# Clearing two DRAM buffers from SyncE's queue in the midst of layer 0's attention in place of GpSimd's, and a later start for GpSimd's gate products

## The chip, the cores and the metric

One core of one Trainium2 chip runs the whole program. The metric is the time of one execution on the device in microseconds (us); of several runs the median counts.

## The reference, cut to what matters

A trunk of two layers works on 512 tokens of 1024 features. Each layer has a mixer, whose three head groups read one normalised input, and a channel mixer: a dense SwiGLU in layer 0, a mixture of 8 experts with 2 chosen per token in layer 1. What matters here is the recurrent head group, whose result is multiplied by a gelu of `y`, and the fact that the experts need rows of memory that are cleared beforehand.

```python
def recurrent_group(x_in, y_in, conv_w, conv_b, wa, ba, wx, bx, lam):
    xc = causal_conv(x_in, conv_w, conv_b)
    return rg_lru(xc, wa, ba, wx, bx, lam) * jax.nn.gelu(y_in)

def mixer(...):
    a_out = recurrent_group(x_lru, y_lru, ...)
    b_out = mla_group(...)            # 6 heads, causal attention
    c_out = nsa_group(...)            # 6 heads, selected and window attention
    return jnp.concatenate([a_out, b_out, c_out], axis=-1) @ w_out

def moe_ffn(x, router_w, wg, wu, wd):
    ...                               # each token goes to its 2 best experts
```

## The kernel before, in words

TensorE (PE), VectorE (DVE), ScalarE (ACT), GpSimd (POOL) and SyncE (SP) each run one list of instructions, written by hand in program order and tied together by semaphores: `signal(...)` raises one, `ready(...)` is what another engine waits for.

**A layer** begins with a stage of projections and small preparatory steps (the table PREPARE), then comes attention, then the output projection (rows with `xT` of DVE line L2316), then the channel mixer. Weights come in chunks of 512 KB: SP loads chunk J into one of two buffers `wstage` (L2544) after DVE has split chunk J-2 (L1885), ACT rounds it into `wring_hi` (L1546), DVE forms the rest `wring_lo` (L1885), and PE multiplies. A chunk can be split only when PE has finished with the chunk three places earlier. In layer 0 the last chunks of the loop, the eight of the output projection, are therefore loaded partly during attention and partly after it.

**Attention** is a series of steps s, each with one or two blocks of 128 query rows for two heads; steps of pairs are named (pair, block of rows). The first steps are (0,1), then (0,0) with (0,2), then (0,3), then (1,3). For each step, by engine:

- PE: `scores(s)`, products of queries and keys (L1387) and the causal mask (L1392); then, for the step three back, transposes of the probabilities (`turn`, L1405) and, when a pair is complete, products with the values (L1435; L1424 those of the compressed keys). `scores(s)` waits for ACT's exponentials of step s-2, `turn` waits for DVE's scaling of its step.
- DVE: `scale(s-2)`, a reciprocal (L2227), a product with the gates (L2238) and one multiplication by a per-row factor for each block (L2245, in place); then `maximum(s)`, a reduction of the scores (L2213 to L2220) that raises the semaphore `nmx`.
- ACT: copies of the transposed blocks to SBUF (L1750), then `exps(s)`, the exponentials (L1739), which wait for `nmx` of step s.

Both `scale(0)` and the maxima of steps 0 and 1 belong to the end of the preparatory stage. From step 2 on each engine walks through the steps in order. The maximum of the fourth step, s = 3, comes after `scale(1)` on DVE, and `scale(2)` follows it.

**GpSimd** has little to do. In each layer it issues four pairs of small transfers (L2482, L2483), then, for the two halves c of `y`, three elementwise products that prepare the gelu: `y*y` (L2489, two inputs), a scaling with an added constant (L2491, one input) and a product with `y` (L2493, two inputs). They wait for `y` and for the scan of the recurrence. ACT takes the results in its steps 7 and 8 of attention (`gelu_tanh`, L1684), DVE finishes the recurrence from its step 9 on. After these products GpSimd issues, in layer 0 alone, the transfers that clear DRAM: ten into `expert_results` (L2499) and nine into `expert_slots` (L2505). Their source is one zeroed piece of SBUF, 256 numbers a partition of `iota`, read again and again. The first waits for `nmx` of step 0. The rest of GpSimd's list are squares of `xT` in the output projection (`early_squares`, L2459 to L2468), and in layer 1 the scatter of tokens into `expert_slots` (L2520), which waits until everything is cleared.

```python
if l == 0:
    pool.wait_ge(*ready("nmx", l, 0, 0))
    ...
pool.wait_ge(*ready("lru_out", l, LC - 1))
...
early_squares((l, "ffn"), lambda k: ready("x_mixed", l, k), l == 1)
```

**SyncE** issues nearly all other transfers, in program order. In the loop over chunks of layer 0 it waits, before each chunk, for the split of the chunk two earlier; between chunks stand small transfers that swap halves of rotated vectors (L2557). During attention itself it has only chunks left. In layer 1 it reloads `iota` after all clearing has landed.

Of the kernel before, what the change touches and what calls it, by code (L numbers as in the profile page):

```python
# [29 lines left out]
P = 128  # L30
T = 512
TT = T // P
DM = 1024
# [18 lines left out]
NE = 8  # L52
# [26 lines left out]
NF = len(FEAT)  # L79
# [90 lines left out]
def trunk(nc, io, known):  # L170
    with ExitStack() as ctx:
# [903 lines left out]
        def experts_sp(sp):  # L1075

            def store(n):
                sp.wait_ge(M["turned"], TURNED[n + 1])
                for h, w in row_halves(CAPS[n]):
                    a = n * YROWS + h * P  # L1080
                    sp.dma_start(results_dram[a:a + w, :], ystage[0:w, h, :]).then_inc(M["stored"], 16)

            def load_rows(n):


                sp.wait_ge(*ready("blank", "slotted"))
                if n >= 4:
                    sp.wait_ge(M["gather_mm"], (n - 1) * KC)
                for h, w in row_halves(CAPS[n]):
                    a = n * YROWS + h * P  # L1090
                    sp.dma_start(slot_rows[n % 2][0:w, h, :],
                                 slots_dram[a:a + w, :]).then_inc(*signal(f"wstage{n % WS}", "slots", n, by=16))

            def chunk_of(expert, f):
                return io["ew"][bass.ds(expert * FC + f, 1)].rearrange("a p n -> p (a n)")

            sp.wait_ge(*ready("order"))
            for G in range(NG):
                n, f = divmod(G, FC)
                if f == 0:  # L1100
                    expert = sp.value_load(order[0:1, n:n + 1], min_val=0, max_val=NE - 1)
                if G == 2:
                    sp.wait_ge(*ready("tok_h", TT - 1))
                    sp.wait_ge(*ready("tok_l", TT - 1))
                if G >= ES:

                    sp.wait_ge(M["lo_ready"], FC + max(G - ES, 1) + 1)
                if G < 2:
                    for p in ((0, 1, 2), (3, 4))[G]:
                        _, part, loaded_ = first_part(p)  # L1110
                        sp.dma_start(ew[:, G, part], chunk_of(expert, G)[:, part]).then_inc(loaded_, 16)
                else:
                    sp.dma_start(ew[:, G % ES, :], chunk_of(expert, f)).then_inc(ew_loaded[G % ES], 16)
                if f == 1 and n >= 2:
                    store(n - 2)
                if f == 3 and n + 1 >= 2 and n + 1 < NE:
                    load_rows(n + 1)
            store(NE - 2)
            sp.wait_ge(M["stored"], STORED[NE - 1])
            sp.wait_ge(*ready("flag"))  # L1120
            over = sp.value_load(flag[0:1, 0:1])
            with sp.If(over > 0):
                sp.wait_ge(M["lo_ready"], FC + NG)
                with sp.Fori(1, ROUNDS) as r:
                    for e in range(NE):
                        n = r * NE + e
                        expert = sp.value_load(order[0:1, e:e + 1], min_val=0, max_val=NE - 1)
                        for f in range(FC):
                            sp.wait_ge(M["lo_ready"], n * FC + FC + last_in(ES, f) + 1)
                            sp.dma_start(ew[:, f % ES, :], chunk_of(expert, f)).then_inc(ew_loaded[f % ES], 16)  # L1130
                        sp.wait_ge(M["turned"], turned_again(n) + NTA)
                        for h, w in row_halves(CAP):
                            sp.dma_start(results_dram[bass.ds(r * CAP + (e * YROWS + CAPS[e] - CAP + h * P), w), :],
                                         ystage[0:w, h, :]).then_inc(M["stored"], 16)
                sp.wait_ge(M["stored"], STORED[NE - 1] + 16 * NHA * (ROUNDS - 1) * NE)
            sp.sem_inc(M["all_stored"], 1)
# [1310 lines left out]
        def _(pool):  # L2447
# [22 lines left out]
            for l in range(DEPTH):  # L2470
                if l > 0:
                    early_squares((l, "mix"), lambda k: (D["y_added"], KC * HALVES + k + 1))

                for s, src in enumerate((kcT, vcT)):
                    if s == 0:
                        pool.wait_ge(*ready("roped", l, "kc", 0))
                    else:
                        pool.wait_ge(*ready("feat", l, feat_index("vc", 0)))
                        pool.wait_ge(*ready("win", l, 0))
                    for g in range(2):  # L2480
                        rows = src[g * HD:(g + 1) * HD, :]
                        pool.dma_start(kcg[0:HD, g, :], rows).then_inc(*signal("kcg", l, s, by=16))  # L2482
                        pool.dma_start(kcg[HD:P, g, 0:T - 1], rows[:, 1:T]).then_inc(*signal("kcg", l, s, by=16))  # L2483
                for c in range(LC):

                    y, u = yl[:, c, :], tmp[:, 2 + c, :]
                    pool.wait_ge(*ready("feat", l, feat_index("y", c)))
                    pool.wait_ge(*ready("lru_step", "scan", l, c))
                    pool.tensor_tensor(u, y, y, ALU.mult).then_inc(*signal("gelu_in", l, c, 0))  # L2489
                    pool.wait_ge(*ready("gelu_in", l, c, 0))  # L2490
                    pool.tensor_scalar(u, u, 0.044715, 1.0, ALU.mult, ALU.add).then_inc(*signal("gelu_in", l, c, 1))  # L2491
                    pool.wait_ge(*ready("gelu_in", l, c, 1))
                    pool.tensor_tensor(u, u, y, ALU.mult).then_inc(*signal("gelu_in", l, c, 2))  # L2493
                if l == 0:
                    pool.wait_ge(*ready("nmx", l, 0, 0))
                    blank = results_dram.rearrange("(p a) d -> p (a d)", p=P).rearrange("p (a n) -> p a n", n=256)
                    for a in range(0, blank.shape[1], 16):
                        n = min(16, blank.shape[1] - a)
                        pool.dma_start(blank[:, a:a + n, :], iota[:, 0:256].unsqueeze(1).broadcast_to([P, n, 256])  # L2499
                                       ).then_inc(*signal("blank", by=16))  # L2500
                    for e in range(2, NE):
                        rows = slots_dram[e * YROWS:e * YROWS + CAPS[e], :].rearrange("r (a n) -> r a n", n=256)
                        for a in range(0, CAPS[e], P):
                            w = min(CAPS[e] - a, P)
                            pool.dma_start(rows[a:a + w], iota[0:w, 0:256].unsqueeze(1)  # L2505
                                           .broadcast_to([w, DM // 256, 256])).then_inc(*signal("blank", by=16))
                pool.wait_ge(*ready("lru_out", l, LC - 1))
                if l == 1:
                    pool.wait_ge(*ready("x_mixed", l, 0))
                    pool.wait_ge(*ready("late_consts"))  # L2510
                    pool.tensor_copy(lowerb, lower[:, :]).then_inc(*signal("counters"))
                    pool.tensor_copy(onesb, ones[:, :]).then_inc(*signal("counters"))
                early_squares((l, "ffn"), lambda k: ready("x_mixed", l, k), l == 1)
            pool.wait_ge(*ready("rows"))
            pool.wait_ge(*ready("blank"))
            for i in range(TT):
                pool.wait_ge(*ready("tok_h", i))
                pool.wait_ge(*ready("tok_l", i))
                for at in (0, TT):
                    pool.indirect_dma_start(slots_dram, bass.IndirectOffsetOnAxis(  # L2520
                        ap=row_index[:, at + i:at + i + 1], axis=0), tok_[:, i, :], None
                        ).then_inc(*signal("blank", "slotted", by=16))
            pool.wait_ge(M["all_stored"], 1)
            pool.wait_ge(M["gather_mm"], NE * KC)
            for i in range(TT):
# [11 lines left out]
        def _(sp):  # L2537
# [9 lines left out]
            def swap_halves(l, n):  # L2547
# [7 lines left out]
                for a in range(0, src.shape[0], 2 * half):  # L2555
                    for x, y in ((a, a + half), (a + half, a)):
                        sp.dma_start(swap[at + x:at + x + half, n % 2, :], src[y:y + half, :]  # L2557
                                     ).then_inc(*signal(f"swapped{n % 2}", l, n, by=16))

            def spread_kpe(l):  # L2560

                sp.wait_ge(*ready("roped", l, "kpe", 0))
                sp.dma_start(kh[NOPE:DQK, :, :], kpe[NOPE:DQK, :].unsqueeze(1).broadcast_to([ROPE, HEADS, T])
                             ).then_inc(*signal("spread", l, "kpe", by=16))
# [19 lines left out]
            for l in range(DEPTH):  # L2584
                for J in range(NW * l + (WR + 1 if l == 0 else WS), NW * (l + 1)):
# [7 lines left out]
                    for n, (name, c) in enumerate(ROPES):  # L2593
                        if j == (1 if name == "kpe" else feat_index(name, c)) + WS + WR:
                            swap_halves(l, n)
                    if j == 4 + WS + WR + 1:
                        spread_kpe(l)
                    if 0 <= j - (5 + WS + WR + 1) < 2:
# [188 lines left out]
```

## Time and profile before

| what | value |
|---|---|
| median of 3 runs | 1330.28 us (1328.93 to 1330.73) |
| the profiled execution, its own time | 1324.21 us |
| its span in the profile | 1322.4 us |
| mean granted TensorE clock, as a share of 2.4 GHz | 0.989 |
| busy: PE, DVE, ACT, POOL | 1267.1, 949.1, 677.8, 130.1 us |
| layer 0: attention | about 128 to 221 us |
| layer 1: attention | about 726 to 816 us |
| moved by DMA | 260.26 MB |

Times in rows are us from the start of the span. A row of a timeline has the start, the duration, the engine, the line, the operation and what ended the idle time before it. A granted clock of 1.00 is 2.4 GHz and 0.50 is 1.2 GHz; a value between them is a mean over a stretch in which both occurred.

### The profile page before, as it was taken

What the parts mean: (1) busy time and instruction counts of PE and PEld (TensorE: products, weight loads), DVE (VectorE), ACT (ScalarE), POOL (GpSimd) and SP (SyncE); (2) the same over time, 40 slices, a digit from 0 to 9 for tenths busy, and PEclk for the clock granted to TensorE, in tenths of its full rate; (3) what the DMA queues carried; (4) which work ended last, traced back from release to release, by engine and by line L of the source; (5) the groups of instructions that cost most, each with busy time, mean ns of one, the idle gap of its engine ahead of it and who ended that gap; (6) DMA issues with size and microseconds to landing.
All of it is one profiled execution on the core that took longest, in us unless ns stands there. A gap on an engine that the chain in (4) does not pass through costs nothing.

```text
span 1322.4 us, 24758 instructions
## 1 busy us (share of the span) xinstructions
PE 1267.1 (96%) x10314; PEld 819.6 (62%) x10375; DVE 949.1 (72%) x1304; ACT 677.8 (51%) x993; POOL 130.1 (10%) x113
## 2 busy tenths in 40 slices
PE   7999999999999999999999999979999999999992
PEld 3457565444444444444457565569979988989981
DVE  7886885886531556334886885688788799989996
ACT  6256774443210333112265774365586687787772
POOL 0011320600000000031011000501200000000002
PEclk9999899999999999999999999999999999999997
DMA  8551881444310443012551000168999999999975
GB/s 272 184 151 35 317 334 60 146 186 149 118 67 0 150 165 148 0 33 103 194 150 35 20 1 21 61 238 325 360 381 376 349 348 398 374 352 398 359 307 208
DMA packets 43134, 260.26 MB, mean 197 GB/s; under 512 B 6522, under 2 KB 7546, under 8 KB 28554
## 3 DMA queue, kind: packets, MB, share of 16 engines
q1 hardware_dynamic: 33626, 224.77, 46.1%
q0 software_dynamic: 8960, 33.26, 7.0%
q8 instruction: 84, 1.38, 0.4%
q10 hardware_dynamic: 432, 0.59, 0.1%
q14 instruction: 32, 0.26, 0.1%
HBM read 218.00 MB, written 33.65 MB: 190 GB/s over the span
## 4 chain that ended last, share of the span: by engine, by line
PE 84%; issue 6%; DVE 4%; DMA 3%; POOL 1%; ACT 1%; SPq 0%; POOLq 0%; DVEq 0%; ACTq 0%
PE bank L1177 20%; PE bank L1178 20%; PE bank L1179 19%; PE bank L1387 5%; PE bank L1435 3%; PE bank L1405 3%; PE bank L727 1%; PE bank L726 1%; PE bank L725 1%; DMA expert_slots<-arena,row_index 1%; PE bank L735 1%; PE bank L737 1%; PE bank L736 1%; POOL expert_slots L2520 1%; PE bank L1242 1%
## 5 line engine op out<-in xcount | busy, mean ns | idle before, releaser
L988 DVE SCALAR_TENSOR_TENSOR arena<-arena 128x3072 f16<-128x3072 f32 x86 | 288.2, 3352 | 10.8 <-ACT arena L842 9.1
L842 ACT ACTIVATE arena<-arena 128x3072 f16<-128x3072 f32 x86 | 237.9, 2767 | 41.1 <-DMA arena<-in_ew 19.5
L1177 PE MATMUL bank<-arena 128*128 128x144 bf16 (+3 forms) x877 | 215.1, 264 | 6.0 <-DVE arena L988 2.7
L1178 PE MATMUL bank<-arena 128*128 128x144 f16 (+3 forms) x878 | 215.4, 264 | 0.1
L1179 PE MATMUL bank<-arena 128*128 128x144 bf16 (+3 forms) x867 | 211.2, 263 | 0.0
L1178 PE MATMUL bank<-hl,wring_hi 128*128 128x512 f16 x352 | 133.4, 379 | 1.5 <-issue 0.6
L1179 PE MATMUL bank<-hh,wring_lo 128*128 128x512 bf16 x341 | 129.2, 379 | 0.0
L1177 PE MATMUL bank<-hh,arena 128*128 128x512 bf16 x338 | 128.1, 379 | 1.0
L1178 PE MATMUL bank<-hl,arena 128*128 128x512 f16 x338 | 128.1, 379 | 0.0
L1177 PE MATMUL bank<-hh,wring_hi 128*128 128x512 bf16 (+1 forms) x333 | 126.3, 379 | 1.0 <-DVE wring_lo L1885 0.5
L1179 PE MATMUL bank<-hh,arena 128*128 128x512 bf16 x319 | 120.9, 379 | 0.0
L1177 PE MATMUL bank<-wring_hi,arena 128*128 128x112 bf16 (+1 forms) x704 | 113.6, 216 | 1.5 <-DVE arena L988 1.5
L1179 PE MATMUL bank<-wring_hi,arena 128*128 128x112 bf16 (+1 forms) x704 | 113.5, 216 | 0.0
L1178 PE MATMUL bank<-wring_lo,arena 128*128 128x112 f16 (+1 forms) x704 | 113.4, 216 | 0.0
L1546 ACT ACTIVATE wring_hi<-wstage 128x1024 f16<-128x1024 f32 x44 | 46.4, 1056 | 116.9 <-PE bank L1179 76.2
L1177 PEld LDWEIGHTS bank<-arena 128*128 128x128 f16 x878 | 85.9, 98 | 30.9 <-DVE arena L988 3.2
L1178 PEld LDWEIGHTS bank<-arena 128*128 128x128 f16 x878 | 85.9, 98 | 22.8 <-issue 0.3
L1179 PEld LDWEIGHTS bank<-arena 128*128 128x128 f16 x878 | 85.9, 98 | 22.4
L1739 ACT ACTIVATE arena<-bank,small 128x256 f32<-128x256 f32 (+3 forms) x144 | 75.1, 545 | 23.7 <-DVE small L2220 13.7
L1562 ACT ACTIVATE arena<-arena 128x512 f32<-128x512 f32 x22 | 13.9, 630 | 135.1 <-DVE arena L1921 135.1
L725 PE MATMUL bank<-arena 128*128 128x144 bf16 (+2 forms) x352 | 74.2, 233 | 2.5 <-DVE arena L1021 2.5
L726 PE MATMUL bank<-arena 128*128 128x144 f16 (+2 forms) x352 | 74.2, 233 | 0.0
(334 smaller groups left out, 2521.2 us busy)
## 6 DMA issues: line engine op xcount, KB each, us to landing
arena<-in_ew SPq DMA_DIRECT2D x86, 1536.0 KB, 9.1
arena<-in_dw SPq DMA_DIRECT2D x22, 1536.0 KB, 6.4
wstage<-in_w_chunk SPq DMA_DIRECT2D x44, 512.0 KB, 3.9
expert_results<-iota POOLq DMA_DIRECT2D x9, 2048.0 KB
arena<-in_cmp_w SPq DMA_DIRECT2D x2, 2048.0 KB, 8.0
arena<-arena SPq DMA_DIRECT2D x60, 64.0 KB, 2.1
expert_slots<-iota POOLq DMA_DIRECT2D x5, 512.0 KB
expert_results<-wstage SPq DMA_DIRECT2D x5, 512.0 KB
```

The costliest lines, as they stand in the source:

```text
L725: pe.matmul(out, hi, a_hi, start=(first and m % 2 == 0), stop=False, skip_group_check=True)
L726: pe.matmul(out, hi, a_lo, start=False, stop=False, skip_group_check=True)
L842: act.activation(ew_hi_[:, G % EP, :], ew[:, G % ES, :], ACT.Copy, scale=SW).then_inc(M["hi_ready"], 1)
L988: dve.scalar_tensor_tensor(out=ew_lo_[:, G % EP, :], in0=ew[:, G % ES, :], scalar=SW, in1=ew_hi_[:, G % EP, :], op0=ALU.mult, op1=ALU.subt ...
L1177: pe.matmul(out, w_hi, x_hi, start=first, stop=False)
L1178: pe.matmul(out, w_hi, x_lo, start=False, stop=False)
L1179: return pe.matmul(out, w_lo, x_hi, start=False, stop=last)
L1387: pe.matmul(score_bank[(2 * s + ab) % 4][:, offset(s, n):offset(s, n + 1)], q, k, start=(n == 0), stop=False)
L1405: mm = pe.transpose(turn_bank[ab][:, offset(s, n) + kb * P:offset(s, n) + (kb + 1) * P], Pt[u % 2][:, ab, OFF[i] + kb * P:OFF[i] + (kb + 1 ...
L1435: mm = pe.matmul(ob[ab * HD:(ab + 1) * HD, kb * P:T], v, turned_row(u % 2, ab, kb), start=(kb == 0 and kind == "mla"), stop=(closes and last))
L1546: act.activation(wring_hi[:, J % WR, :, :], wstage[:, J % WS, :, :], ACT.Copy, scale=SW).then_inc(*signal("w_hi", J))
L1739: act.activation(Pt[u % 2][:, ab, OFF[i]:OFF[i] + (i + 1) * P], score_bank[(2 * s + ab) % 4][:, offset(s, n):offset(s, n + 1)], ACT.Exp, b ...
```

## The change

Three edits. SyncE issues the nineteen clearing transfers, in a new function `clear_rows`, after chunk 17 (counted in the order of layer 0) and ahead of the wait for chunk 18. They wait only for the zeros, which are written at the start of the program. GpSimd no longer issues them. And GpSimd's gelu products, in both layers and for both halves, wait in addition for `nmx` of step 3. The scatter's transfers raise a semaphore of their own, `slotted`, instead of sharing `blank`.

```diff
             def load_rows(n):
-                sp.wait_ge(*ready("blank", "slotted"))
+                sp.wait_ge(*ready("slotted"))
...
                 for c in range(LC):
                     y, u = yl[:, c, :], tmp[:, 2 + c, :]
+                    pool.wait_ge(*ready("nmx", l, 3, 0))
                     pool.wait_ge(*ready("feat", l, feat_index("y", c)))
                     pool.wait_ge(*ready("lru_step", "scan", l, c))
                     pool.tensor_tensor(u, y, y, ALU.mult).then_inc(*signal("gelu_in", l, c, 0))
...
-                if l == 0:
-                    pool.wait_ge(*ready("nmx", l, 0, 0))
-                    blank = results_dram.rearrange("(p a) d -> p (a d)", p=P).rearrange("p (a n) -> p a n", n=256)
-                    for a in range(0, blank.shape[1], 16):
-                        n = min(16, blank.shape[1] - a)
-                        pool.dma_start(blank[:, a:a + n, :], iota[:, 0:256].unsqueeze(1).broadcast_to([P, n, 256])
-                                       ).then_inc(*signal("blank", by=16))
-                    for e in range(2, NE):
-                        ...
                 pool.wait_ge(*ready("lru_out", l, LC - 1))
...
+            def clear_rows():
+                sp.wait_ge(*ready("by_pool", "zeros"))
+                blank = results_dram.rearrange("(p a) d -> p (a d)", p=P).rearrange("p (a n) -> p a n", n=256)
+                for a in range(0, blank.shape[1], 16):
+                    n = min(16, blank.shape[1] - a)
+                    sp.dma_start(blank[:, a:a + n, :], iota[:, 0:256].unsqueeze(1).broadcast_to([P, n, 256])
+                                 ).then_inc(*signal("blank", by=16))
+                for e in range(2, NE):
+                    rows = slots_dram[e * YROWS:e * YROWS + CAPS[e], :].rearrange("r (a n) -> r a n", n=256)
+                    for a in range(0, CAPS[e], P):
+                        w = min(CAPS[e] - a, P)
+                        sp.dma_start(rows[a:a + w], iota[0:w, 0:256].unsqueeze(1)
+                                     .broadcast_to([w, DM // 256, 256])).then_inc(*signal("blank", by=16))
...
                     for n, (name, c) in enumerate(ROPES):
                         ...
+                    if l == 0 and j == NF + WR + 1:
+                        clear_rows()
...
                     chunk(J)
```

GpSimd's list in layer 0, from its last gelu product to the squares of the output projection. Before, with what each instruction waits for:

```order
L2489 TENSOR_TENSOR arena<-arena 128x512 [waits lru_step,feat]
L2491 TENSOR_SCALAR arena<-arena 128x512 [waits gelu_in]
L2493 TENSOR_TENSOR arena<-arena 128x512 [waits gelu_in]
L2499 DMA expert_results<-iota 128x16x256 [waits nmx]
L2499 DMA expert_results<-iota 128x16x256 x8
L2499 DMA expert_results<-iota 128x4x256
L2505 DMA expert_slots<-iota 512x1x256
L2505 DMA expert_slots<-iota 160x1x256
```

And with the change:

```order
L2490 TENSOR_TENSOR arena<-arena 128x512 [waits lru_step,feat,nmx]
L2492 TENSOR_SCALAR arena<-arena 128x512 [waits gelu_in]
L2494 TENSOR_TENSOR arena<-arena 128x512 [waits gelu_in]
L2459 TENSOR_TENSOR arena<-xT 128x512 [waits x_mixed,lru_out]
L2463 TENSOR_TENSOR arena<-xT 128x512 [waits x_mixed]
```

The transfers are gone from this list, and the first product of each half has one more semaphore to wait for. The lists of PE, DVE and ACT are the same as before.

SyncE's list from the last swap of halves in layer 0 to its end; `wstage<-in_w_chunk` are the chunks of weights. Before:

```order
L2557 DMA arena<-arena 32x512 [waits roped,feat]
L2557 DMA arena<-arena 32x512 x3
L2544 DMA wstage<-in_w_chunk 128x1024 [waits w_lo] x6
L2625 UNCONDITIONAL_BRANCH [waits lru_out,pv]
L2625 ISA
```

And with the change:

```order
L2532 DMA wstage<-in_w_chunk 128x1024 [waits w_lo] x2
L2554 DMA expert_results<-iota 128x16x256 [waits by_pool]
L2554 DMA expert_results<-iota 128x16x256 x8
L2554 DMA expert_results<-iota 128x4x256
L2560 DMA expert_slots<-iota 512x1x256
L2560 DMA expert_slots<-iota 160x1x256
L2560 DMA expert_slots<-iota 448x1x256
L2560 DMA expert_slots<-iota 512x1x256
L2560 DMA expert_slots<-iota 64x1x256
L2560 DMA expert_slots<-iota 512x1x256 x2
L2532 DMA wstage<-in_w_chunk 128x1024 [waits w_lo] x4
```

Two of the six chunks now come ahead of the nineteen transfers and four behind them.

## Rows read from the trace of the kernel before

**Rows 1.** The page's chain that ended last, shares of the span by engine.
```profile
PE 84%; issue 6%; DVE 4%; DMA 3%; POOL 1%; ACT 1%; SPq 0%; POOLq 0%; DVEq 0%; ACTq 0%
```
**Rows 2.** Stretches: us; PE, PEld, DVE, ACT, POOL busy; clock, DMA share, GB/s.
```profile
128.00:148.90 20.90, 18.61 (x95) 9.89 (x96) 17.07 (x34) 12.87 (x40) 13.09 (x12) 0.84 0.60 226
726.10:744.10 18.00, 16.59 (x95) 8.45 (x96) 14.75 (x34) 11.92 (x39) 4.35 (x5) 1.00 0.07 26
148.89:218.66 69.77, 69.31 (x469) 42.24 (x472) 54.27 (x131) 49.82 (x154) 9.36 (x12) 1.00 0.74 274
744.09:813.86 69.77, 69.31 (x469) 42.25 (x472) 53.66 (x131) 50.88 (x157) 0.00 (x0) 1.00 0.03 8
```
**Rows 3.** The chain of waits, layer 0, two pieces: start, us, what.
```profile
128.05 1.08 PE bank L1387 x8
...
148.89 1.33 PE bank L1435 x5
```
**Rows 4.** The chain of waits, layer 1, the same stage.
```profile
726.17 1.08 PE bank L1387 x8
...
732.82 1.28 DVE small L2238
...
734.12 1.14 DVE arena L2245 x4
...
744.09 2.09 PE bank L1435 x11
```
**Rows 5.** Timeline of layer 0, DVE and POOL at the third step.
```profile
134.69 1.27 POOL L2493 TENSOR_TENSOR arena<-arena 128x512 f32<-128x512 f32 x1
134.71 1.27 DVE L2238 TENSOR_TENSOR small<-small,arena 128x4 f32<-128x4 f32 x1
...
135.90 8.64 POOL L2499 DMA_DIRECT2D expert_results<-iota  x7
...
136.01 2.48 DVE L2245 TENSOR_SCALAR arena<-arena,small 128x128 f32<-128x128 f32 x4
```
**Rows 6.** Timeline of layer 1, third to fifth step, POOL, DVE and ACT.
```profile
730.97 1.04 POOL L2489 TENSOR_TENSOR arena<-arena 128x512 f32<-128x512 f32 x1 [3.37 <-DVE arena L1995]
...
732.10 0.62 POOL L2491 TENSOR_SCALAR arena<-arena 128x512 f32<-128x512 f32 x1
...
736.51 0.16 DVE L2238 TENSOR_TENSOR small<-small,arena 128x2 f32<-128x2 f32 x1
736.70 0.88 DVE L2245 TENSOR_SCALAR arena<-arena,small 128x512 f32<-128x512 f32 x2
...
737.50 1.28 DVE L2220 TENSOR_REDUCE small<-bank 128x2 f32<-128x256 f32 x2
...
737.77 1.07 ACT L1750 COPY arena<-bank 128x512 f32<-128x512 f32 x2
...
738.88 0.37 ACT L1739 ACTIVATE arena<-bank,small 128x128 f32<-128x128 f32 x1
```
**Rows 7.** Timeline of layer 0's output projection, DVE and POOL.
```profile
231.08 1.21 DVE L1885 SCALAR_TENSOR_TENSOR wring_lo<-wstage,wring_hi 128x1024 f16<-128x1024 f32 x1
...
231.24 1.95 POOL L2463 TENSOR_TENSOR arena<-xT 128x512 f32<-128x512 f32 x1 [2.42 <-DVE xT L2316]
232.22 1.52 DVE L2290 SCALAR_TENSOR_TENSOR arena<-xT,gains,arena 128x512 f16<-128x512 f32 x1
```
**Rows 8.** Timelines of layer 0: ACT's rounding of chunk 18, SP's chunk 17.
```profile
228.58 1.04 ACT L1546 ACTIVATE wring_hi<-wstage 128x1024 f16<-128x1024 f32 x1
...
126.71 0.33 SPq L2544 DMA_DIRECT2D wstage<-in_w_chunk  x1
```
**Rows 9.** DMA from 127 to 210 us: queue, packets, MB, share.
```profile
q0 software_dynamic: 5888, 22.78, 73.8%
```
**Rows 10.** Stretches as in Rows 2: the first clearing, and preparation in layer 1.
```profile
137.00:175.00 38.00, 36.21 (x241) 21.47 (x240) 32.73 (x79) 28.85 (x90) 7.54 (x7) 0.91 1.00 377
...
707.00:711.00 4.00, 4.00 (x24) 2.79 (x24) 2.84 (x5) 1.19 (x2) 0.00 (x0) 0.60 0.00 0
```

More of the change, by code:

```diff
@@ L2493, in _ @@
                     pool.tensor_tensor(u, u, y, ALU.mult).then_inc(*signal("gelu_in", l, c, 2))
-                if l == 0:
-                    pool.wait_ge(*ready("nmx", l, 0, 0))
-                    blank = results_dram.rearrange("(p a) d -> p (a d)", p=P).rearrange("p (a n) -> p a n", n=256)
-                    for a in range(0, blank.shape[1], 16):
-                        n = min(16, blank.shape[1] - a)
-                        pool.dma_start(blank[:, a:a + n, :], iota[:, 0:256].unsqueeze(1).broadcast_to([P, n, 256])
-                                       ).then_inc(*signal("blank", by=16))
-                    for e in range(2, NE):
[L2502 to L2506, printed above, removed]
                 pool.wait_ge(*ready("lru_out", l, LC - 1))
@@ L2521, in _ @@
                         ap=row_index[:, at + i:at + i + 1], axis=0), tok_[:, i, :], None
-                        ).then_inc(*signal("blank", "slotted", by=16))
+                        ).then_inc(*signal("slotted", by=16))
             pool.wait_ge(M["all_stored"], 1)
```

## The prediction

> **What bounds the kernel now.** I read the page's chain first: TensorE makes up 84% of it [rows 1], so a change on GpSimd and in the queues counts only where PE waits for somebody. Then the chain in order of time shows where that is near the change: at the start of attention. The two layers run the same lists there, and before the change only layer 0 has the clearing transfers, so the trace holds its own comparison. From the scores of the second step to the first products with values layer 0 takes 148.89 - 128.05 = 20.84 us [rows 3] and layer 1 takes 744.09 - 726.17 = 17.92 us [rows 4]: 2.92 us more in layer 0. In the 69.77 us behind that, the two layers are equal to the hundredth, with the DMA engines 74% busy in one and 3% in the other, and 12 of GpSimd's instructions in the one and none in the other [rows 2]. So PE hides there what DVE and ACT lose, and DMA traffic as such costs nothing. All the change can give, and take, lies in the short first stretch, where PE waits for DVE's chain: scaling, maximum, then ACT's exponentials.
>
> In that stretch three things are seen. First, in both layers DVE's tiny product L2238 (4 numbers a partition) lasts 1.27 us or 1.28 us at the third step, exactly beside GpSimd's last product L2493, which began 0.02 us earlier [rows 4, 5]; one step later the like instruction lasts 0.16 us [rows 6]. Second, in layer 0 the next four multiplications L2245 last 2.48 us while GpSimd issues clearing transfers [rows 5], against 1.14 us in layer 1 [rows 4]. Third, the granted clock is 0.84 in layer 0's stretch, so PE ran part of it at 1.2 GHz, against 1.00 in layer 1 [rows 2]; PE had stood waiting just ahead of that.
>
> **The change, part by part.**
>
> *The clearing off GpSimd.* What layer 0 loses against layer 1 goes: 2.92 us. Of it 2.48 - 1.14 = 1.34 us is the stall of four instructions; the rest are smaller stalls of the same kind and the low clock that followed the wait. I take the whole 2.92 us; the lower end is 1.3 us, if the clock falls there all the same.
>
> *The clearing on SP.* The nineteen transfers are issued right after chunk 17, at about 127.0 us [rows 8], ten us earlier than now. They move 22.78 MB [rows 9]. At the 377 GB/s of the first clearing [rows 10] that is 60 us, so they end near 187 us. SP is the only engine held up, and behind the transfers in its list stand the last four chunks. The first of them, chunk 18, is rounded by ACT at 228.58 us [rows 8]. The cover is thus 228.58 - 127.04 = 101.5 us, and the queue must keep up 22.78 / 101.5 = 224 GB/s. Priced at nothing. If the cover fails, the output projection waits for its weights (see the rivals). Attention itself needs no transfer in that time. The scatter in layer 1 waits for the clearing, which lies some 700 us earlier.
>
> *The products no longer beside the third step.* DVE's L2238 falls from 1.27 to about 0.17 us in both layers, and the maximum of step 3 comes 1.10 us earlier.
>
> *The products beside the fourth step.* They now start with that maximum. In layer 1's old times: L2238 of the next scaling starts at 736.51 us now [rows 6], so at 736.51 - 1.10 = 735.41 us then, and the maximum ends some 0.1 us ahead of it. Two engines start at once: GpSimd with L2489, 1.04 us long [rows 6], and DVE with `scale(2)`, that is L2238 of 0.16 us and two L2245 of 0.88 us together, whose end lets the maximum of step 4 begin [rows 6]. Where two such instructions meet, one waits for the whole of the other: at the output projection GpSimd's L2463 stands behind DVE's L1885 and takes 1.95 us in place of the 1.04 of its like, and DVE's L2290 in turn stands behind it and takes 1.52 us [rows 7]. The waiting engine got its turn between two instructions of the other. So DVE is held here for about one product, 1.05 us. The open question is the second product, L2491, 0.62 us [rows 6]. It starts some 0.1 us after the first ends, between DVE's two L2245. If it holds DVE as well, what is left of DVE's first L2245 runs beside its wait and the sum of the delay is about 1.47 us. L2493 then falls beside the maximum L2220, which reads PSUM; the trace shows the reduction at its usual 1.2 us beside products before, so nothing is charged.
>
> What that does to the chain: without any delay the exponentials of step 4 could start at 737.78 us, which is 738.88 - 1.10, since ACT's copies L1750 move forward too. With a delay of DVE d the maximum of step 4 ends at 737.50 + 1.28 - 1.10 + d = 737.68 + d, and they start some 0.05 us later, at 737.73 + d, or at 737.78 if that is later. They start at 738.88 us now [rows 6]. So d = 1.05 gives 738.78, a gain of 0.1 us a layer, d = 1.47 gives 739.20, a loss of 0.3 us, and d = 0 gives 1.1 us. I take the middle of the two likely ones, a loss of 0.1 us a layer; that is, the old stall at the third step is exchanged for one of the same size at the fourth. The bounds are a gain of 1.1 and a loss of 0.5 us a layer.
>
> The Trainium skill speaks against the change here (page "SBUF — State Buffer", section "Who interferes with whom"): a VectorE instruction in a two-port mode, `tensor_scalar` among them, and any GpSimd instruction exclude each other for their whole length, as do two-input VectorE instructions and GpSimd ones that read SBUF. By that rule L2491 does hold L2245, and the sum would be 2.92 - 0.6 = 2.3 us in place of 2.7. No row of this trace has a one-input GpSimd product beside such a DVE instruction.
>
> *The second half's products* follow on the first's and meet `scale(3)` and `scale(4)`, which they may hold by up to two us. By then PE has transposes and, from 744.09 us on [rows 4], the long products with values to do; it waits for nobody there, and what DVE loses stays under that cover, as in rows 2. If the cover were gone, the price would be those two us a layer. ACT takes the products' results only in its steps 7 and 8, three steps on: no cost.
>
> *The semaphore of its own* for the scatter: the last increments are the same ones. Nothing.
>
> **The sum**, for the profiled execution: 2.92 - 2 x 0.1 = 2.7 us, so 1324.21 becomes 1321.5 us. The median of the runs stands 6.07 us above that execution; nothing in the trace says why, and I carry the difference over: 1330.28 - 2.7 = 1327.6 us. 0.2% is 2.66 us here, about what a measurement of this kernel tells from no change, and the forecast lies right at that bound.
>
> **The rivals.**
>
> A. *The moved products hold nobody that matters* (GpSimd reaches them late, or DVE's small instructions slip through). Then both layers gain the 1.10 us of the third step: 2.92 + 2.20 = 5.1 us, 1325.2 us. For it: a DVE reduction from PSUM is not touched. Against it: `scale(2)` begins within a tenth of a us of the products. Chance 0.10.
>
> B. *The clock.* In layer 1 a stretch ahead of attention shows a clock of 0.60 over 4 us [rows 10]: 3.2 us at 1.2 GHz, worth 1.6 us of PE's work. Layer 0 has nothing like it at the same work. Such a stretch can go when all later work shifts by 2.7 us: gain 4.3 us, 1326.0 us, chance 0.09. Or one more can come, or the one in layer 0 can stay: gain 1.1 us, 1329.2 us, chance 0.13.
>
> C. *The change does not remove the stall*: the four slow L2245 are slow for another reason than GpSimd's issuing. Then 0 to 0.3 us, 1330.2 us. Against it: the two layers differ in nothing else. Chance 0.03.
>
> D. *Slower: SP's queue becomes the bound.* The queue has one order, and chunks 18 to 21 stand behind 22.78 MB cut into pieces of 1 KB at the source. The decisive point is 224 GB/s. At 200 GB/s the clearing ends at 127 + 114 = 241 us and chunk 18 lands at least 12.5 us after it is wanted: 1330.28 + 12.5 - 2.7 = 1340.1 us. For it: no row shows this queue with such pieces. Against it: the same addresses took 377 GB/s from the other queue. Chance 0.05.
>
> **How the numbers follow.** The forecast case has 0.60 (both signs of the second product's effect in it, so 1327.2 to 1328.0 us), and it splits about evenly at the 0.2% bound: 0.32 above, 0.28 within. Faster by over 0.2%: 0.32 + 0.10 (A) + 0.09 (B) = 0.51. Within 0.2%: 0.28 + 0.13 + 0.03 = 0.44. Slower: 0.05 (D). The range reaches from A to a little above the bad side of B, as the runs before spread over 1.8 us: 1325.2 to 1329.9 us. It leaves out D, C and the tails.
>
> **What would show it.** In the new profile's layer 0 the four L2245 ahead of the fourth step's maximum last 1.14 us and the clock is 1.00 over the first stretch; from L1387 x8 to L1435 it takes 18.0 us in both layers. L2238 at the third step lasts 0.17 us. At the fourth step L2238 or L2245 lasts a us or more too long, beside L2490. SP's transfers move from 127 to about 187 us, and chunk 18 lands before 228 us. I am wrong in the mechanism if DVE shows no stall at the fourth step, or if layer 0 stays slower than layer 1 there; wrong in the cover if ACT waits for `wstage` at the output projection.

## The result and the profile after

The changed kernel takes 1336.72 us (median of 5 runs, 1335.15 to 1337.77). The kernel before, run beside it, takes 1329.56 us (5 runs, 1328.48 to 1330.73). The ratio is 1.006, 95% interval 1.0044 to 1.0075. Slower by 7.2 us, where 2.7 us faster was forecast, and outside the range.

The two profiled spans differ by more, 12.5 us (1334.9 against 1322.4), because the profiled execution of before was a quick one. I split both spans at the same instructions: the *opening* of attention is the time from the scores of the second step (L1387 x8) to the second group of value products (the second L1435 x16), so that all that PE waits for is in it.

| stretch | before | after | difference |
|---|---|---|---|
| start to layer 0's opening | 128.05 | 127.67 | -0.4 |
| opening, layer 0 | 30.34 | 33.22 | +2.9 |
| between the openings | 567.78 | 567.83 | 0 |
| opening, layer 1 | 27.42 | 33.07 | +5.7 |
| from there to the end | 568.8 | 573.1 | +4.3 |

The last row is not taken to be the change's: a second profile of the unchanged kernel (below) has 571.9 us there, and the eight experiments' profiles lie between 570 and 575 us whether they are faster or slower than before. What remains is 8.5 us in the two openings, where the median moved by 7.2 us (5.9 to 10.0 us by the interval).

The chain of waits of the changed kernel through layer 1's opening answers to [rows 4]; columns are start, us, what:

```profile
728.72 1.07 PE bank L1387 x8
...
735.38 0.18 DVE small L2238
...
735.58 1.14 DVE arena L2245 x4
736.72 1.13 DVE small L2213
...
737.96 1.04 DVE small L2238
...
739.02 2.34 DVE arena L2245 x2
741.37 1.21 DVE small L2220 x2
...
742.66 1.03 ACT arena L1739 x4
...
743.73 2.98 PE bank L1387 x3
...
747.04 1.71 PE bank L1405 x8
748.75 1.90 PE bank L1424 x4
750.65 3.95 PE bank L1435 x16
```

Up to the maximum of the fourth step (L2213 at 736.72) everything is as forecast: L2238 is down to 0.18 us, the four L2245 last 1.14 us. Then L2238 lasts 1.04 us and the two L2245 last 2.34 us in place of 0.16 and 0.88 [rows 6]. And from 743.73 us on PE's own work is stretched: the transposes L1405 x8 take 1.71 us where they took 0.88, the values L1424 1.90 where they took 1.00. Its timeline at the fourth step shows who holds whom:

```profile
737.94 1.04 POOL L2490 TENSOR_TENSOR arena<-arena 128x512 f32<-128x512 f32 x1 [60.95 <-DVE small L2213]
737.96 1.03 DVE L2238 TENSOR_TENSOR small<-small,arena 128x2 f32<-128x2 f32 x1
...
739.02 2.34 DVE L2245 TENSOR_SCALAR arena<-arena,small 128x512 f32<-128x512 f32 x2
...
739.07 0.61 POOL L2492 TENSOR_SCALAR arena<-arena 128x512 f32<-128x512 f32 x1
739.76 1.32 POOL L2494 TENSOR_TENSOR arena<-arena 128x512 f32<-128x512 f32 x1
...
743.73 2.13 PE L1387 MATMUL bank<-arena 64*128 64x512 f32 x3 [1.59 <-ACT arena L1739]
```

The two L2245 of that row, taken by themselves (shortest, median and longest in ns, first and last start):

```profile
L2245 DVE TENSOR_SCALAR arena<-arena,small x2: 942/1212/1482, 739.0 to 739.9; 128x512 f32<-128x512 f32 x2
```

GpSimd's three products each hold DVE once: L2490 holds L2238, L2492 the first L2245 (0.94 us; it ends 0.28 us after L2492), L2494 the second (1.48 us; it ends 0.28 us after L2494). PE then waits 1.59 us in one piece. The stretches of the changed kernel, columns as in [rows 2], show the clock; the first row is layer 0 and ends in the midst of its slow piece, the other two are layer 1 before and after its clock fell:

```profile
128.00:148.90 20.90, 18.04 (x90) 9.03 (x88) 18.39 (x37) 12.95 (x40) 6.04 (x6) 0.86 1.05 370
...
738.00:743.90 5.90, 3.54 (x27) 2.57 (x26) 5.79 (x8) 3.54 (x12) 5.55 (x6) 0.98 0.00 0
743.90:754.10 10.20, 10.20 (x30) 4.16 (x32) 6.30 (x15) 6.15 (x17) 0.42 (x1) 0.51 0.17 53
```

PE was busy for 3.54 of 5.90 us, and then ran 10 us at 1.2 GHz with no wait left in them. In [rows 2] layer 1's clock in this stage was 1.00. It is no matter of one execution: the mean clock of the whole program was 0.979 to 0.981 in all five executions of the changed kernel, and 0.985 to 0.992 in the 24 of the kernel before that ran beside the last experiments.

The clearing itself went as forecast. The stretch from 126.7 us on, with DMA share and rate as the last two columns:

```profile
126.70:190.00 63.30, 60.44 (x369) 32.88 (x369) 51.87 (x121) 43.64 (x136) 6.04 (x6) 0.92 1.06 374
```

And two rows of its timelines, SyncE's issue of chunk 18 and ACT's rounding of it:

```profile
185.66 1.44 SPq L2532 DMA_DIRECT2D wstage<-in_w_chunk  x1
...
231.08 1.04 ACT L1546 ACTIVATE wring_hi<-wstage 128x1024 f16<-128x1024 f32 x1
```

The transfers run at 374 GB/s, chunk 18 is issued at 185.66 us and rounded at 231.08 us with no wait for it.

### The profile page after: what moved, and what is told of

Read it like the earlier page. It is cut to its first block, busy times and chain, and to the rows that moved or that the text cites. A ratio compares the mean times of both kernels' runs of the same rounds, so it can differ in the third digit from the quotient of the medians.

```text
span 1334.9 us, 24819 instructions
## 1 busy us (share of the span) xinstructions
PE 1281.2 (96%) x10375; PEld 823.5 (62%) x10375; DVE 951.0 (71%) x1304; ACT 678.8 (51%) x993; POOL 113.5 (9%) x94
## 4 chain that ended last, share of the span: by engine, by line
PE 85%; issue 6%; DVE 4%; DMA 3%; POOL 2%; ACT 1%; SPq 0%; POOLq 0%; DVEq 0%; ACTq 0%
PE bank L1177 20%; PE bank L1178 19%; PE bank L1179 19%; PE bank L1387 4%; PE bank L1435 3%; PE bank L1405 3%; PE bank L727 1%; PE bank L726 1%; PE bank L725 1%; DMA expert_slots<-arena,row_index 1%; PE bank L735 1%; PE bank L737 1%; PE bank L736 1%; POOL expert_slots L2508 1%; PE bank L1242 1%
## 5 line engine op out<-in xcount | busy, mean ns | idle before, releaser
L1177 PE MATMUL bank<-arena 128*128 128x144 bf16 (+3 forms) x878 | 215.5, 264 | 5.7 <-DVE arena L988 3.0
L1179 PE MATMUL bank<-arena 128*128 128x144 bf16 (+3 forms) x878 | 215.4, 264 | 0.0
L1177 PE MATMUL bank<-hh,wring_hi 128*128 128x512 bf16 x352 | 133.5, 379 | 0.5 <-DVE wring_lo L1885 0.4
L1179 PE MATMUL bank<-hh,wring_lo 128*128 128x512 bf16 x352 | 133.4, 379 | 0.0
L1179 PE MATMUL bank<-hh,arena 128*128 128x512 bf16 x338 | 128.1, 379 | 0.0
L1177 PE MATMUL bank<-hh,arena 128*128 128x512 bf16 x338 | 128.1, 379 | 0.0
L1387 PE MATMUL bank<-arena 64*128 64x256 f32 (+7 forms) x288 | 71.1, 469 | 4.2 <-ACT arena L1739 4.2
```

The costliest lines, as they stand in the source:

```text
L1177: pe.matmul(out, w_hi, x_hi, start=first, stop=False)
L1179: return pe.matmul(out, w_lo, x_hi, start=False, stop=last)
L1387: pe.matmul(score_bank[(2 * s + ab) % 4][:, offset(s, n):offset(s, n + 1)], q, k, start=(n == 0), stop=False)
```

## The experiments

Eight kernels, in two groups of four as in the order below; those of one group share their runs of the kernel before (median 1328.68 us for the first four, 1327.98 us for the last four). Opening is the stretch defined above, from each kernel's own profile.

| kernel | ratio to before, 95% interval | opening, layer 0 | layer 1 |
|---|---|---|---|
| before (first profile) | 1 | 30.34 | 27.42 |
| changed | 1.006 (1.0044 to 1.0075) | 33.22 | 33.07 |
| before again | 0.9998 (0.9987 to 1.0009) | 29.20 | 27.42 |
| clearing on SyncE alone | 0.9972 (0.9956 to 0.9989) | 27.42 | 27.43 |
| late products alone | 1.006 (1.0043 to 1.0077) | 33.36 | 33.15 |
| products at the seventh step | 0.9957 (0.9940 to 0.9973) | 27.09 | 27.10 |
| second half after the sixth step | 0.9959 (0.9941 to 0.9976) | 26.31 | 26.31 |
| changed, PE's wait filled | 0.9986 (0.9972 to 1.0001) | 28.66 | 28.65 |
| changed, short second product | one execution, 1336.06 us | 33.12 | 33.06 |
| GpSimd clears from the seventh step | 0.9975 (0.9961 to 0.9988) | 27.42 | 27.42 |

The theory after the result was: the clearing's move is good, the wait does all the harm; of the harm the larger part is TensorE's clock. Rivals: SyncE's transfers do harm; attention varies by itself.

**The kernel before again.** No edit.

> The kernel before, unchanged, for a second profile of it. Its profiled execution (1324.21 us) stood 5 us under the median of its runs, so a part of the 12.5 us between the two profiled spans has nothing to do with the change. Theory: the time is about 1329.5 us (ratio 1.000), attention looks as in the first profile (20.8 us and 17.9 us for the first stretch of the layers), and the 4 to 5 us come from behind layer 1's attention. Rival: attention itself varies from one execution to the next, and then the 8.5 us of the two attentions cannot be laid to the change.

Median 1328.32 us, ratio 0.9998. Layer 1's opening is 27.42 us to the hundredth; layer 0's is 29.20, 1.1 us less than in the first profile. The DVE stall is there again (2.48 us for the four L2245 in the chain, from 137.55 us on), but the clock stayed up:

```profile
128.00:148.90 20.90, 17.94 (x100) 8.85 (x98) 17.11 (x36) 13.04 (x42) 14.52 (x13) 1.00 0.55 200
```

So of the 2.92 us that the prediction took from layer 0, 1.8 us are DVE's stall, there in both profiles (1.34 us on the four L2245 and 0.44 us on the next two), and 1.1 us are a fall of the clock that one profile has and the other has not. Why it comes in one and not in the other, the rows do not say. The same stretch of work in the first and in the second profile, with PE as busy in one as in the other, and last what followed in the first:

```profile
134.00:140.20 6.20, 4.19 (x28) 2.56 (x26) 6.06 (x11) 2.54 (x7) 6.12 (x6) 1.00 0.39 156
135.54:141.74 6.20, 4.18 (x28) 2.55 (x26) 6.06 (x11) 2.54 (x7) 6.12 (x6) 1.00 0.39 156
140.20:147.00 6.80, 6.52 (x22) 3.87 (x23) 5.64 (x16) 6.33 (x21) 4.34 (x4) 0.50 1.02 379
```

So behind this wait the clock may fall or stay. In these two profiles the openings vary by no more than that, the time ahead of them by 1.5 us (129.59 against 128.05 us) and the time behind them by 3.1 us (571.9 against 568.8 us).

**The clearing on SyncE alone.**

```diff
                 for c in range(LC):
-                    pool.wait_ge(*ready("nmx", l, 3, 0))
                     pool.wait_ge(*ready("feat", l, feat_index("y", c)))
```

> The change without its wait: SyncE clears, GpSimd's products start as before. Theory 1 (the wait at the fourth step did all the harm, and moving the transfers is good): DVE's four L2245 in layer 0 last 1.14 us, layer 0's first stretch shrinks by 2.9 us to 17.9 us, ratio about 0.998 (2 to 3 us faster than before). Rival (SyncE's transfers themselves do harm): slower than before, layer 0's attention longer than layer 1's.

Median 1323.82 us beside 1328.68, ratio 0.9972. Both layers have the same opening now:

```profile
127.66:155.08 27.42, 26.01 (x167) 14.39 (x168) 22.01 (x53) 19.02 (x63) 4.43 (x5) 1.00 1.06 371
721.24:748.67 27.43, 26.03 (x167) 14.40 (x168) 22.03 (x53) 19.03 (x63) 4.43 (x5) 1.00 0.11 37
```

Layer 0 runs it beside saturated DMA engines (share 1.06) and layer 1 beside idle ones, in the same time. The rival falls: SyncE's transfers do no harm.

The ratio amounts to 3.7 us, and the openings explain 1.8 us of it (2.9 us against the first profile). Another 1.6 us lie between the openings, which take 566.17 us here and 567.8 us in every profile above: the slow piece ahead of layer 1's attention, 0.60 in [rows 10], is absent.

```profile
700.00:720.00 20.00, 19.92 (x168) 14.15 (x167) 15.84 (x30) 16.32 (x25) 1.17 (x1) 1.00 0.00 1
```

It is absent in the last experiment too (566.16 us) and present in the six others. Whether moving the clearing alone brings this about, or chance, two profiles do not show.

**The late products alone.** Against the kernel before:

```diff
                 for c in range(LC):
+                    pool.wait_ge(*ready("nmx", l, 3, 0))
                     pool.wait_ge(*ready("feat", l, feat_index("y", c)))
```

> The wait alone: products from the fourth step on, GpSimd still clears behind them. Theory 1: in both layers DVE is held by 2.3 us at the fourth step and the clock falls for some 10 us, so attention takes about 5.7 us longer in layer 1, and in layer 0 at least as much: 9 to 12 us slower than before, ratio 1.007 to 1.009. Rival (the harm comes from SyncE's transfers): within 2 us of before.

Median 1337.36 us, ratio 1.006, openings 33.36 and 33.15 us: the changed kernel's time without its other part. The expectation was 9 to 12 us, and it came to 8.7 us; layer 0 lost less than I added up, since GpSimd's clearing waits behind its products (its first transfer is issued at 145.03 us in this kernel) and now falls where PE waits for nobody. That also shows why the clearing's move bought nothing inside the change: the late products had already moved it out of the way.

**The products at the seventh step.** Against the changed kernel:

```diff
-                    pool.wait_ge(*ready("nmx", l, 3, 0))
+                    pool.wait_ge(*ready("nmx", l, 6, 0))
```

> The change, but the products wait for the maximum of the seventh step (s = 6) in place of the fourth. Theory 1 (what counts is whether PE waits for DVE at that point): no stall at the third or the fourth step, PE is busy with values by the seventh, so the 1.1 us of the third step are gained in both layers on top of the 2.9 us: about 5 us faster than before, ratio 0.996. Rival (a product costs wherever it meets DVE): no better than the change without its wait.

Median 1322.89 us, ratio 0.9957. The time came as expected, but not by the way that was expected. The opening shrinks by only 0.33 us against the clearing alone, not by 1.1 us. The stall of the third step is gone and one of the eighth has come, as its chain shows:

```profile
144.34 2.06 DVE wring_lo L1885
...
146.91 2.50 DVE arena L2245 x2
149.42 1.21 DVE small L2220 x2
...
150.71 1.03 ACT arena L1739 x4
...
151.78 2.04 PE bank L1387 x8
```

"PE is busy with values by the seventh" was a share of busy time, not a place in the chain. Against the first profile of before, the two openings give 3.6 us of the 5.8 us by which the medians differ (3.6 to 8.0 us by the interval). The rest is in no row, and that the ratio met the expected 0.996 may be luck.

**The second half after the sixth step.** Against the changed kernel; the first half's products start as in the kernel before:

```diff
-                    pool.wait_ge(*ready("nmx", l, 3, 0))
+                    if c == 1:
+                        pool.wait_ge(*ready("pn", l, 5, 1, 0))
```

> SyncE clears; the first half's products start as in the kernel before (there DVE stands idle for over 2 us), and only the second half's three products wait, for the end of DVE's scaling of the sixth step (s = 5), behind which DVE stood idle for 2 us and then reads PSUM. Theory 1 (a product costs only where DVE has a two-input or tensor_scalar instruction on the way to a waiting PE): the 1.1 us of the third step are gained in both layers and nothing is paid at the seventh or eighth, so 2 x 1.1 us faster than the clearing on SyncE alone, 5 to 7 us faster than before, ratio about 0.9955 or less, and up to 1.5 us better than the products at the seventh step. Rival: DVE is then late for the steps after it, and nothing is gained over the products at the seventh step.

Median 1323.86 us beside 1327.98, ratio 0.9959. The timeline of its layer 0 behind the sixth step's scaling:

```profile
148.24 0.62 DVE L2245 TENSOR_SCALAR arena<-arena,small 128x256 f32<-128x256 f32 x2
...
148.94 1.04 POOL L2491 TENSOR_TENSOR arena<-arena 128x512 f32<-128x512 f32 x1 [17.19 <-DVE arena L2245]
150.06 0.62 POOL L2493 TENSOR_SCALAR arena<-arena 128x512 f32<-128x512 f32 x1
150.77 1.28 POOL L2495 TENSOR_TENSOR arena<-arena 128x512 f32<-128x512 f32 x1
152.09 0.15 DVE L2227 RECIPROCAL small<-small 128x2 f32<-128x2 f32 x1
152.27 0.16 DVE L2238 TENSOR_TENSOR small<-small,arena 128x2 f32<-128x2 f32 x1
```

The three products fit where DVE is idle or reads PSUM (`bank` in the rows), and hold nobody. The openings are 26.31 us, 1.11 us under the clearing alone in both layers, the whole of the third step's stall. The openings put it 1.6 us ahead of the products at the seventh step; the ratios cannot tell the two apart. Both beat the two kernels of this study. The gain over the kernel before is 0.4%.

**The changed kernel with PE's wait filled.**

```diff
-SPARE = {}
+SPARE = {6: 8}
```

> The changed kernel with eight superfluous products of 128x512 (bf16) on TensorE ahead of the scores of step 6, where it stands idle for 1.6 us waiting for the exponentials; they write a bank that is cleared by the next product and change no result. Theory 2 (of the 5.7 us that layer 1's attention loses, 1.2 us are the wait and the rest is the clock, which falls to 1.2 GHz for 10 us because PE stood idle): the clock stays at 2.4 GHz, and about 4 us a layer come back, so about 8 us faster than the changed kernel, ratio to before 0.999 to 1.001. Rival (the stall itself makes all of the loss): as slow as the changed kernel or slower, ratio 1.006.

Median 1326.93 us, ratio 0.9986, its interval just reaching 1. By the ratios it is 9.8 us faster than the changed kernel, and the two openings give 9.0 us. DVE's stall is untouched (L2245 x2 takes 2.35 us) and PE's scores still wait for it; but in that wait it now does useless work, and the clock stays up, as its stretches in layer 1 show:

```profile
733.00:738.90 5.90, 5.13 (x35) 3.30 (x34) 5.76 (x10) 3.35 (x11) 5.31 (x6) 1.00 0.01 3
739.00:749.20 10.20, 10.20 (x69) 5.47 (x69) 8.62 (x21) 7.97 (x23) 0.63 (x1) 1.00 0.18 51
```

Against 3.54 of 5.90 us busy in the changed kernel it is 5.13 of 5.90, and PE gets through 69 matmuls in the next 10.2 us where it got through 30. Its chain has the same work as the last rows of the changed kernel's chain above:

```profile
739.18 1.90 PE bank L1387 x4
...
741.29 0.88 PE bank L1405 x8
742.17 1.00 PE bank L1424 x4
743.18 2.31 PE bank L1435 x16
```

These four take 6.09 us in place of 10.54. The opening falls from 33.07 to 28.65 us in layer 1: 4.4 us of its 5.65 us loss were the clock, 1.2 us the wait (28.65 - 27.42), of which about 0.1 us is the filler itself running past the gap. In all ten executions of this kernel the mean clock was 0.987 or more. So the rival falls that the stall makes all of the loss.

**The changed kernel with a short second product.**

```diff
-                    pool.tensor_scalar(u, u, 0.044715, 1.0, ALU.mult, ALU.add).then_inc(*signal("gelu_in", l, c, 1))
+                    pool.tensor_scalar(u[:, 0:8], u[:, 0:8], 0.044715, 1.0, ALU.mult, ALU.add
+                                       ).then_inc(*signal("gelu_in", l, c, 1))
```

> The changed kernel with GpSimd's one-input product (tensor_scalar) on 8 of its 512 columns, so that it is nearly gone; the scaling inside the gelu is left out for the other columns. Theory 3 (each of the three products holds DVE for its own length, the one-input one too): the first of DVE's two L2245 behind the fourth maximum no longer waits 0.46 us, the pair takes about 1.9 us or less in place of 2.35, and the exponentials of step 4 start about 0.5 us earlier. Rival (only the two-input products hold DVE): the pair still takes 2.35 us.

This kernel leaves out the scaling inside the gelu for all but 8 of the 512 columns, so its result is not the reference's; only its rows are of use, from one execution. Its timeline of layer 0 at the fourth step, DVE and POOL:

```profile
138.50 1.93 DVE L2245 TENSOR_SCALAR arena<-arena,small 128x512 f32<-128x512 f32 x2
...
138.54 0.19 POOL L2492 TENSOR_SCALAR arena<-arena 128x8 f32<-128x8 f32 x1
138.81 1.33 POOL L2494 TENSOR_TENSOR arena<-arena 128x512 f32<-128x512 f32 x1
```

The pair by itself, as for the changed kernel above:

```profile
L2245 DVE TENSOR_SCALAR arena<-arena,small x2: 520/1006/1492, 138.5 to 138.9; 128x512 f32<-128x512 f32 x2
```

The pair takes 1.93 us in place of 2.35, and all of the difference is in the first of the two (0.52 us in place of 0.94; the second takes 1.49 against 1.48): the one-input product does hold DVE for its own length, and the two-input one behind it holds the second. The opening hardly changes (33.12 and 33.06 us), since the clock falls all the same; half a microsecond less of stall is not what decides that.

**GpSimd clears, from the seventh step.** Against the kernel before:

```diff
                 if l == 0:
-                    pool.wait_ge(*ready("nmx", l, 0, 0))
+                    pool.wait_ge(*ready("nmx", l, 6, 0))
```

> The kernel before with one number changed: GpSimd issues the clearing itself, but waits for the maximum of the seventh step (s = 6) in place of the first. Theory 4 (it is the moment of GpSimd's issuing, beside DVE's scaling while PE waits, that costs layer 0 its 1.8 to 2.9 us, not the queue): as fast as the clearing on SyncE alone, ratio about 0.998, four L2245 at 1.14 us in layer 0. Rival (issuing on GpSimd costs wherever it stands): no faster than before, ratio 1.000.

Median 1325.32 us, ratio 0.9975, opening 27.42 us in both layers. The clearing on SyncE gives no more (0.9972). What cost layer 0 its time was the moment at which GpSimd issued, not the queue. As with the clearing on SyncE, 1.6 us of the gain in the profile lie between the openings.

## Why the prediction was wrong, by its own steps

**What bounds the kernel: right.** All that moved lies in the openings; between them the two kernels agree within 0.05 us.

**The clearing off GpSimd: right in kind, and 1.1 us larger than the second profile has it.** The stall of L2245 is gone. I took 2.92 us from one profile; the second profile shows 1.8 us of it without any fall of the clock. By itself the part is worth 0.28% (0.11 to 0.44%), and in its profile 1.6 us of that are the missing slow piece ahead of layer 1's attention. Rival B had named such a case, gave it 0.09, and no row tells whether it is an effect of the part or chance.

**The clearing on SP: right.** Nothing, at 374 GB/s, with over 40 us to spare. The slower rival D, the only one on that side, was the wrong one.

**The third step's L2238: right**, 0.18 us in both layers.

**The products beside the fourth step: the step that failed.** It held the delay d to be 1.05 to 1.47 us, on the ground that GpSimd's third product "falls beside the maximum L2220, which reads PSUM". It did not. The first L2245, which L2492 had delayed, ran until 739.96 us, and the third product had been issued at 739.76 us, so it had its turn between the two, and the second L2245 took 1.48 us. Measured: 0.87 us on L2238, and 2.34 - 0.88 = 1.46 us on the pair, d = 2.3 us. The maximum came behind that. By the prediction's own formula, 737.73 + 2.3 is 740.0 us, 1.2 us later than 738.88, and 1.2 us is what the filled kernel shows. Rows 7 held the pattern (the waiting engine gets its turn between two instructions); I used it for the second product and dropped it for the third. The rule of the Trainium skill (page "SBUF — State Buffer", section "Who interferes with whom"), which would hold L2245 behind the one-input product too, is borne out by the short product: 2.35 us became 1.93. I had written it down and then priced half of it.

**The clock: the term that made the size.** Rival B treated the clock as chance, one stretch of 3 us worth 1.6 us. In layer 0 of the kernel before it did fall in one profile and not in the other. In the changed kernel it is a consequence: the wait, 1.2 us longer, leaves PE busy for 3.54 of 5.90 us, the clock falls, and the 10 us behind it are PE's own work, which gives little back. It fell in both layers of all three profiles with this wait (the changed kernel, the late products alone, the short product), and in neither layer once the wait was filled. 4.4 us a layer, against 1.2 us for the wait. The prediction had counted a low clock behind a wait for the clearing (0.84 in layer 0, rows 2), but priced the new wait only by when ACT could start, and put at nothing what PE's standing idle would do to the work behind it. And the two openings together explain the result: 2 x 5.65 us lost, less the 1.8 to 2.9 us that layer 0 had lost before anyway, is 8.4 to 9.5 us, near the measured 7.2 us and the 8.7 us of the late products alone.

**The second half's products: right enough.** They held `scale(3)` by about a microsecond, and nothing in the chain shows it.

What stays open: why the 570 us behind layer 1's opening vary by up to 6 us from profile to profile, and what brings or removes the slow piece ahead of layer 1's attention. No run here was aimed at either.

## What to carry to other kernels

When a helper engine's work is moved, follow it instruction by instruction against the engine that its instructions were seen to hold: every one of its operations can take a turn, also between two of the other's, and the sum counts, not the first. Put it where the other engine is idle or reads PSUM, and look for that place in the chain, not in busy shares. And price a wait of TensorE twice: its own length, and the clock of the work behind it if it comes just ahead of a long stretch in which PE is the bound; there, useless matmuls in the gap were worth 4.4 us in each layer. Moving the products so that the wait never arose was worth more (26.31 against 28.65 us).

## What the runs showed of the hardware that I had not expected

The fall of the clock costs more than the wait that brings it: 1.2 us of waiting, 10.2 us at 1.2 GHz, 4.4 us lost, in each layer. With 5.13 us of 5.90 busy in place of 3.54 it did not fall. A chain of three GpSimd instructions, 3.0 us in all, held three DVE instructions of 0.16, 0.44 and 0.44 us for 2.3 us. And while transfers cut into 1 KB pieces from a broadcast source went out from SyncE's queue, the DMA engines moved 374 GB/s.
